# Two experts for 64 tokens in each gathered slot, and their weighted sums on two column groups of TensorE

## What is computed

```python
q = (hb @ wq).reshape(blk, P_HEADS, P_QDIM)
s1 = jnp.einsum('thd,nd->thn', q[..., :P_HALF], k1)
s2 = jnp.einsum('thd,nd->thn', q[..., P_HALF:], k2)
v1, i1 = lax.top_k(s1, P_TOPK)
v2, i2 = lax.top_k(s2, P_TOPK)
...
sc, pos = lax.top_k(cand, P_TOPK)
eidx = jnp.take_along_axis(cidx, pos, axis=-1)
g = jax.nn.softmax(sc, axis=-1)
act = jax.nn.gelu(jnp.einsum('td,thkd->thk', hb, u[eidx]), approximate=False)
return jnp.einsum('thk,thkd->td', (g * act), v[eidx])
```

## Time and profile before

| | us |
|---|---|
| median of 3 runs | 2501.39 |
| lowest and highest | 2500.70, 2506.66 |
| the profiled execution | 2500.45 |
| its span, first to last instruction | 2498.7 |

### The profile page before, as it was taken

How to read it: one execution, slowest core, us unless ns; L and a number is a source line. 1 busy time by engine, 2 the same in 40 slices (tenths; PEclk the granted TensorE clock), 3 DMA queues, 4 the chain that set the end, 5 groups by cost and what they waited for, 6 DMA issues and landing times.

```text
span 2498.7 us, 25279 instructions
## 1 busy us (share of the span) xinstructions
PE 2168.8 (87%) x9074; PEld 1251.7 (50%) x9074; DVE 1228.3 (49%) x3177; ACT 764.2 (31%) x2200; POOL 734.8 (29%) x694
## 2 busy tenths in 40 slices
PE   6999989997799879999997878787879787978786
PEld 3777438874588545555553433343334333433221
DVE  1000001216233146566566766767676766676864
ACT  2000012242132034444234443343333333333322
POOL 0000001110102013434333535344434343435351
PEclk8999989997699989999998989898989898989899
DMA  9566648988686649999999999999999999999997
GB/s 355 224 250 236 249 151 306 329 315 325 252 306 223 224 183 390 391 404 399 393 389 394 420 398 400 419 416 409 420 419 413 420 418 412 382 420 420 420 420 299
DMA packets 125490, 875.53 MB, mean 350 GB/s; under 512 B 15945, under 2 KB 17257, under 8 KB 40501
## 3 DMA queue, kind: packets, MB, share of 16 engines
q0 software_dynamic: 85760, 691.32, 68.7%
q1 hardware_dynamic: 38652, 182.48, 19.3%
q10 hardware_dynamic: 952, 0.13, 0.0%
HBM read 861.53 MB, written 99.37 MB: 385 GB/s over the span
## 4 chain that ended last, share of the span: by engine, by line
PE 35%; DVE 14%; DMA 13%; ACT 2%; issue 2%; POOL 0%; ACTq 0%; POOLq 0%; DVEq 0%
PE ps L1868 24%; DMA pr_ring<-in_uv,pr_idx 12%; PE ps L1764 3%; DVE pr_ring L2090 3%; PE ps L1804 3%; PE ps L1813 1%; PE ps L1826 1%; PE ps L1786 1%; DVE pr_hot L2074 1%; DVE pr_hot L2070 1%; DVE pr_ind L2051 1%; DVE pr_ind L2048 1%; DVE pr_pick L2077 1%; DVE pr_val L2050 1%; ACT pr_coef L1940 1%
## 5 line engine op out<-in xcount | busy, mean ns | idle before, releaser
L1868 PE MATMUL ps<-pr_ring,pr_diag 128*128 128x512 f32 (+1 forms) x2224 | 1042.4, 623 | 209.6 <-ACT pr_diag L1944 209.4
L1749 POOL DMA_INDIRECT pr_ring<-in_uv,pr_idx x556 | 640.6, 1152 | 956.0 <-PE ps L1868 812.0
L2090 DVE CUSTOM_DVE_ANT_0 pr_ring<-pr_ring,h 128x1024 f32<-128x1024 f32 x556 | 662.7, 1224 | 353.6 <-DMA pr_ring<-in_uv,pr_idx 351.2
L1868 PEld LDWEIGHTS ps<-pr_ring,pr_diag 128*128 128x128 f32 (+1 forms) x2224 | 424.4, 195 | 772.9 <-issue 476.7
L1935 ACT ACTIVATE pr_gel<-pr_dots 128x2 f32<-128x2 f32 x288 | 58.0, 201 | 521.7 <-DVE pr_dots L2090 521.0
L1944 ACT ACTIVATE pr_diag<-ident,pr_coef 128x128 f32<-128x128 f32 x512 | 173.5, 386 | 0.0
L1940 ACT ACTIVATE pr_coef<-pr_gel,pr_wgt 128x1 f32<-128x1 f32 x576 | 138.4, 287 | 27.0 <-ACT pr_gel L1935 0.4
L1764 PE MATMUL ps<-trunk,pr_wq 128*128 128x320 f32 (+2 forms) x544 | 132.1, 397 | 3.0 <-ACT trunk L1970 2.2
L465 PE MATMUL ps<-trunk,ap_ring 128*128 128x288 f32 x384 | 126.5, 411 | 2.9 <-PEq L192 2.9
L379 DVE TENSOR_TENSOR late_rows<-ps,late_bias 128x512 f32<-128x512 f32 x2 | 1.4, 692 | 253.0 <-PE ps L369 253.0
L466 PE MATMUL ps<-trunk,ap_ring 128*128 128x288 f32 x384 | 125.6, 409 | 0.0
(11 more groups left out here) (316 smaller groups left out, 2255.5 us busy)
## 6 DMA issues: line engine op xcount, KB each, us to landing
out_win_s<-in_cache POOLq DMA_DIRECT2D x64, 1020.0 KB, 7.9
sa_ring<-in_cache SPq DMA_DIRECT2D x24, 1024.0 KB, 9.4
side_unit<-in_w_merge SPq DMA_DIRECT2D x32, 768.0 KB
late_ring<-in_w_ada SPq DMA_DIRECT2D x8, 2048.0 KB, 17.3
sa_ring<-in_kcacheB SPq DMA_DIRECT2D x16, 1024.0 KB, 7.7
pr_wq<-in_peer_wq SPq DMA_DIRECT2D x16, 1024.0 KB
out_win_s<-in_cache POOLq DMA_DIRECT2D x16, 1008.0 KB, 9.8
ap_ring<-in_w_attn_qk SPq DMA_DIRECT2D x6, 2048.0 KB, 21.2
```

The source lines that it names most:

```text
L1749: pool.indirect_dma_start(row(n), None, d["uv"], bass.IndirectOffsetOnAxis(ap=idx[:, b % 4, j:j + 1], axis=0)).then_inc(arrived[slot(n)], 16)
L1868: mm = pe.matmul(ps[0:r, bank + half, :], diag[:, slot(n), 0:r], row(n)[:, o:o + CHUNK], start=h == 0 and j == 0, stop=b == FINAL[i] and j ...
L2090: ins = dve.tensor_tensor_reduce(u, u, e.h2[:, BLOCKS[b][0], :], 1.0, 0.0, ALU.mult, ALU.add, dots[:, slot(n):slot(n) + 1])
```

## The change

A slot of a prompt tile no longer holds one expert for 128 tokens. It holds two experts for 64 tokens: an even slot serves the tokens of partitions 0 to 63, an odd one those of 64 to 127; partitions 0 to 63 of the slot get the first expert and 64 to 127 the second. Indices and weights are written in that order by four instructions each, for the four pairs of token half and expert half (`PAIRS`). For the dot products the input rows must lie in the same order, so `e.pair` holds, for each of two tiles at a time, the rows of either token half twice. SyncE makes these by copies within SBUF: three for each of tiles 0 and 1, after the rows are made and turned, and four for each of tiles 2 and 3, once the dots of the tile before in that place are done. `e.h2` keeps only tiles 2 to 4.

The diagonal becomes the folded one, 128x64, for all tiles, and the product of a slot writes the 64 PSUM partitions of its token half. TensorE now takes a pair at a time: it waits for both diagonals, and issues for each half of the columns the product of the even slot (PSUM partitions 0 to 63) and then that of the odd one (64 to 127). The number of slots, their bytes, and the number and width of the matmul instructions stay.

For room, half of the query weights moves into `trunk` (rows of 1 KB, and two DMAs in place of one), later queries move too, and the scores, the candidates and the one-hot rows are placed beside the diagonals.

```diff
 def load_query_weights(sp, d, e, r):
-    sp.dma_start(e.wq[:], d["peer_wq"][r % PH]).then_inc(e.wq_ready, 16)
+    for half in range(2):
+        sp.dma_start(e.wq[half], d["peer_wq"][r % PH][:, half * KD // 2:(half + 1) * KD // 2]).then_inc(e.wq_ready, 16)
...
+HALF = P // 2
...
+PAIRS = [(slice(side * HALF, (side + 1) * HALF), slice(part * HALF, (part + 1) * HALF), slice(side, TOPK, 2),
+          slice(part * TOPK // 2, (part + 1) * TOPK // 2)) for side in range(2) for part in range(2)]
...
+                for i in range(GROUP):
+                    sp.wait_ge(s_h2, i + 1)
+                    for o in (HALF, 0):
+                        sp.dma_start(e.pair[o:o + HALF, 2 * i + 1, :], e.pair[HALF:P, 2 * i, :]).then_inc(s_pair[i], 16)
+                    sp.wait_ge(s_tr, i + 1)
+                    sp.wait_ge(s_pair[i], 32)
+                    sp.dma_start(e.pair[HALF:P, 2 * i, :], e.pair[0:HALF, 2 * i, :]).then_inc(s_pair[i], 16)
                 sp.wait_ge(s_q, query_count(1, 0))
                 load_query_weights(sp, d, e, 1)
...
                 for g in range(PER * FINAL[PT]):
+                    b, q = divmod(g, PER)
+                    if q == 0 and b - 1 in (FINAL[0], FINAL[1]):
+                        i = BLOCKS[b - 1][0]
+                        sp.wait_ge(s_dot, PER * b)
+                        for half in range(2):
+                            for o in (0, HALF):
+                                sp.dma_start(e.pair[o:o + HALF, 2 * i + half, :],
+                                             e.h2[half * HALF:(half + 1) * HALF, i, :]).then_inc(s_pair[i + GROUP], 16)
...
                     for q in range(PER):
-                        for j in range(q * BATCH, (q + 1) * BATCH):
-                            n = b * TOPK + j
-                            pe.wait_ge(s_dg, n + 1)
+                        n = b * TOPK + q * BATCH
+                        if i < PT:
+                            pe.wait_ge(s_dg, n + BATCH)
                             for half in range(2):
                                 o = D + half * CHUNK
-                                mm = pe.matmul(ps[0:r, bank + half, :], diag[:, slot(n), 0:r],
-                                               row(n)[:, o:o + CHUNK], start=h == 0 and j == 0,
-                                               stop=b == FINAL[i] and j == TOPK - 1)
-                            mm.then_inc(s_v, 1)
+                                for side in range(2):
+                                    mm = pe.matmul(ps[side * HALF:(side + 1) * HALF, bank + half, :],
+                                                   diag[:, slot(n + side), :], row(n + side)[:, o:o + CHUNK],
+                                                   start=h == 0 and q == 0, stop=h == PH - 1 and q == PER - 1)
+                                    if half == 1:
+                                        mm.then_inc(s_v, 1)
...
-                        act.activation(diag[:, o + j, 0:r], k.ident[:] if i < PT else k.fold[:], ACT.Copy,
+                        act.activation(diag[:, o + j, :], k.fold[:], ACT.Copy,
...
+                    if BLOCKS[b][0] < PT:
+                        for src, dst, to, js in PAIRS:
+                            dve.scalar_tensor_tensor(idx[dst, b % 4, to], pick[src, 0, js], float(NKEYS), pick[src, 1, js],
+                                                     ALU.mult, ALU.add)
+                        dve.wait_ge(s_ex, b + 1)
+                        chain.step(dve.reciprocal(rex[:], exs[:]))
+                        for src, dst, to, js in PAIRS:
+                            ins = dve.tensor_scalar(wgt[dst, b % 4, to], ex[src, js], rex[src], None, ALU.mult)
+                        ins.then_inc(s_idx, 1)
...
                 def dots_of(b, q):
+                    i, h = BLOCKS[b]
+                    if h == 0 and q == 0 and i < PT:
+                        dve.wait_ge(s_pair[i], 48 if i < GROUP else 64)
...
-                        ins = dve.tensor_tensor_reduce(u, u, e.h2[:, BLOCKS[b][0], :], 1.0, 0.0, ALU.mult, ALU.add,
+                        rows = e.pair[:, 2 * (i % GROUP) + j, :] if i < PT else e.h2[:, PT - GROUP, :]
+                        ins = dve.tensor_tensor_reduce(u, u, rows, 1.0, 0.0, ALU.mult, ALU.add,
                                                        dots[:, slot(n):slot(n) + 1])
...
-        e.x1, e.h2, e.h2T = sb("x1", [P, NCH, D]), sb("h2", [P, NCH, D]), trunk[:, KD:, :]
-        e.wq = sb("pr_wq", [P, KD, 2 * P])
+        e.x1, e.h2T = sb("x1", [P, NCH, D]), trunk[:, KD:, :]
+        e.pair, e.h2 = sb("h2_pair", [P, 2 * GROUP, D]), sb("h2_rest", [P, NCH - GROUP, D])
+        e.wq = [sb("pr_wq", [P, KD // 2, 2 * P])[:], trunk[:, 4:KD, 0:GROUPED]]
```

58 lines of the change are left out of this document (35 added, 23 removed).

## The result

The changed kernel takes 2522.53 us in the median (2517.96 to 2527.65), the kernel before 2501.05 on the same chip. The ratio is 1.0099, with a 95% interval of 1.0073 to 1.0125: 25 us slower by the ratio, between 18 and 31, where 11 us faster was forecast. The profiled execution took 2517.96 us, with a span of 2516.2.

What follows compares the result with a forecast made beforehand. TensorE was taken to bound 950 to 1300 us (48.6 against 46.2 us a block), the DMA the late stage. Terms -15 (first stretch), -6 (dips), +1 (routing), +7 (copies), +2 (1 KB runs) gave -11: 2490 us, range 2474 to 2511.

Steps and rivals of the forecast that it cites:

- the copies: Input-row copies on SyncE's queue, eleven of them in the full queue: 0.65 us each, 7 us lost, bounds 7 and 40.
- the slipped load: The load issued at 926.73 us, just behind tile 1's copies: some us of slip, once, under a full ring.
- The first stretch: 950 to 1300 us, TensorE-bound: overlap makes the DMA the bound at 415 GB/s, 15.2 us gained, bounds 7 and 19.
- D: Rival: the column groups don't overlap, no gain and 10 us of cost, 2511 us; chance 0.05.
- rival C: Copies and 1 KB runs in a saturated DMA outweigh the freed TensorE, 2510 to 2520 us; chance 0.11.
- Routing: VectorE's added instructions, 1.0 us a block, lie beside transfers later; only the first block's 1.0 us is exposed.
- The later dips: Rate dips such as at 1360 and 2170 us: cheaper pairs clear backlogs sooner, 6 us gained, bounds 0 and 16.
- rival B: TensorE's clock falls with its work and the dips stay: gain 6 us less, about 2496 us; chance 0.10.
- Diagonals and order: Pairs wait 0.3 us for the second diagonal, the first slot comes free some 0.4 us later: zero, hidden under queued transfers.
- A: Rival: only the idle share returns, the first stretch's low rate being the side loads' own; 2498 to 2503 us, chance 0.15.
- E: Rival: all the lost DMA time is returned, about 2475 us; chance 0.10 with what lies between.
- F: Rival: the copies run at half the rate, using half the partitions' ports: 14 us for eleven, 2497 us; chance 0.06.

Runs made afterwards that it cites:

- e2: Changed kernel with both products of a pair on one column group, so the two cannot overlap: ratio 1.0191 to the kernel before, 23 us above the changed kernel.
- e16: Changed kernel with late copies on ScalarE, query weights in 4 KB runs, and routing's index and weights by one instruction each: ratio 0.9974 to the kernel before.
- e11: e8 with two further unread matmuls behind each pair of blocks 13 to 31: ratio 1.0048 to the kernel before, 14 us above e8.
- e6: Kernel before, waiting for both diagonals of a pair and taking products half by half, as in the changed one: ratio 1.0049, 12 us slower.
- e8: Changed kernel with late copies on ScalarE and query weights in 4 KB runs: ratio 0.9992 to the kernel before, 27 us below the changed kernel.
- e15: Changed kernel with late and tile 1's copies on ScalarE, 4 KB runs, routing in three pieces, second diagonal awaited only at its first matmul: ratio 0.9954, 2488.23 us.

## Why the prediction was wrong

What failed first of all is the price of the added traffic. I had 7 us for the copies, 2 for the 1 KB runs and nothing for the slipped load; taking out the late copies and the runs gave back 27 us (18 to 35), the whole of the slowdown.

*The first stretch: right.* -15 was forecast. 20.3 us came in blocks 1 to 7, 14 at equal bytes, with a pair of 1.94 us, 1.86 from start to next start (950.31 to 952.17), where 1.72 was taken from the four-group row. "TensorE below 80% busy" was 84%; the rate is 415 GB/s between those gathers, but 404 in the window of 950 to 1300, where I had asked for 410. D (no overlap) is out: e2 costs 23 us.

*Copies: mis-sized.* 0.65 us each, measured 1.6 to 1.9, for the eight late ones some 13 us (5 to 21) instead of 5. The upper bound of 3.6, from a single copy in disturbed company, was too high. I had taken the lower end since the rows beside it could explain the loss; a single pair of copies in a saturated queue would have been needed to say so. This is rival C's mechanism, by the middle values at less than the 2.4 us a copy from which I had let it decide; the rest came from the terms below.

*The slipped load: mis-sized.* "Some us of slip, once, under a ring that is then full" was priced at nothing: 13.2 us of wait, 9 us in block 0. The place was named exactly, the cover not looked at: the ring is full, but of slots that only the waiting TensorE can free.

*1 KB runs: no contradiction alone, wrong together.* 2 us forecast, 2 measured in the kernel before (error 5, so that nothing would fit as well), 11 in the changed one (error 8), more than half of it this one load by the profile.

*Routing: mis-placed.* 1.0 us a block was 1.24; "later they lie beside transfers" was wrong, 5 to 7 us in three runs instead of 1.

*The later dips: wrong.* I took 6 us, on the ground that a pair at half the price clears a backlog in half the time. The ground held: 3.68 against 6.78 us behind a wait, four pairs in 9.27 against five in 20.08. The gain did not come with it. e16 has neither late copies nor 1 KB runs, and a routing as short as before; still its blocks 8 to 35 take 1174.7 us against 1161.8, some 10 of the 12.9 being bytes that earlier blocks no longer carry, and 3 on top. Its line for blocks 8 to 15:

```profile
1276.34:1628.61 352.27, 207.78 (x720) 74.31 (x718) 241.39 (x591) 132.85 (x412) 144.38 (x129) 0.77 1.00 399
```

So clearing the backlog sooner did not shorten the dips by what I took; e16 still has the changed order and the joint wait, which can hide a part. The waits themselves went from 221 to 499 us in all; much of that is only a TensorE that is done sooner, but the routing that makes the long ones is VectorE's, as the prediction said and then didn't count. That the dips stay and the clock falls (0.75 to 0.79 in blocks 8 to 27) is what rival B had, with 0.10. Its cause isn't shown: with the clock raised in e11, blocks 18 to 27 were not shorter.

*Diagonals and order: not settled.* I had named the joint wait and the later release, and costed both at zero. In the kernel before they cost 12 us together; in the changed one only the wait could be tried (4 us, error 7).

*The other rivals.* A is out: the rate of blocks 1 to 7 rose to 415 GB/s, so it was TensorE that held it. E too, by the time (its costs are 10 us by my own terms, not 9). F's half rate, 1.25 us a copy, lies within the run's interval and below the windows' value. D's price is the plainest sign: I gave the change without the overlap 10 us of cost, and e2, which keeps part of the overlap, stands 48 us above the kernel before. Late copies and runs (27), tile 1's copies (2.5), routing (6) and e6's order and wait (12) come to about as much. The errors are too wide to call that shown, but it points to the costs (10) and not to the gain (21, where e2 has 23 or more, a part of them perhaps the 12 of the order taken back).

*Sum.* Forecast -15 - 6 + 1 + 7 + 2 = -11. By the runs: +25 for the changed kernel, less 27 for late copies and runs, is -2 for e8; less 9.5 for tile 1's copies, the routing in three pieces and the single waits is -11.5 for e15. That this equals the forecast is chance: e15 no longer has the 7 + 2, so that my terms give -20 for it. Of the error of 36 us some 25 are named: the copies, the slipped load and the runs (27 + 2.5 where I had 9, 20 us) and the routing (5 to 7 where I had 1, 5 us). The other 11 lie between the dips, which brought no gain where I had 6, and the order within a pair, at zero; how they share, and how much of the routing's 5 to 7 us and the 3 us of the split is in the same dips, is open.

## What to carry to other kernels

When a second bound lies just under the first (here 46.2 against 48.6 us a block), a faster engine can win only the gap, and every byte, run and wait that the change adds can land on the new bound at full price: count them as exposed unless a row shows cover. A load that slips while the ring is full is not covered by the ring if the engine waiting for it is the one that frees the slots. Rearranging on chip is better done by an engine with slack than by a copy in a saturated DMA queue: here eight of the fourteen copies of 256 KB, put on ScalarE, gave back 13 us (5 to 21), more than half of the 23 that e2 shows for the column groups; three more gave 2.5, within the error.

## What the hardware showed that I had not expected

- Two float32 column groups of 64 columns run side by side: 1.94 us for eight matmuls of 512 columns, against 3.65 us on one group at the same clock. At half the clock it is 3.68 against 6.78.
- Behind four copies of 256 KB (64 partitions each) within the chip's SBUF the DMA went from 419 to 252 GB/s over 10 us at a share of 1.03: a full share says little of the rate.
- The same 1 KB runs cost 2 us (error 5) in one kernel and 11 (error 8) in another; more than half of the 11 lies at one load with copies ahead of it.
- Blocks 18 to 27 took 423.54 us at a granted clock of 0.77 and 423.51 at 0.90, the latter with two more matmuls behind most pairs (one execution each).
